# Odd layer of a nine-layer forward pass: gate products in two half units, late scans inside attention steps, rotary rows in tiles of their own

## The reference, cut to what matters

```python
def odd_mixer(h, w_in, g_cq, w_uq, g_ckv, w_ukv, conv_w, conv_b, wa, ba, wx, bx, lam, w_out):
    cq, ckv, kr, xr, xg = np.split(h @ w_in, ...)      # 256, 128, 32, 512, 512 columns
    q = (rmsnorm(cq, g_cq) @ w_uq).reshape(Bsz, S, 8, 64 + 32)
    qn, qr = q[..., :64], rope_2(q[..., 64:])
    kv = (rmsnorm(ckv, g_ckv) @ w_ukv).reshape(Bsz, S, 8, 64 + 64)
    yc = dense_mla(qn, qr, kv[..., :64], rope_2(kr), kv[..., 64:])   # full softmax attention
    yd = rglru_block(xr, xg, conv_w, conv_b, wa, ba, wx, bx, lam)
    return jnp.concatenate([yc, yd], axis=-1) @ w_out

def rglru_block(...):
    xc = conv_b + sum_j conv_w[j] * xp[:, j:j + S]     # 4 taps
    for dirn in range(2):
        r, i = sigmoid(xc @ wa[dirn] + ba), sigmoid(xc @ wx[dirn] + bx)   # block-diagonal, 64 wide
        log_a = -8 * r * softplus(-lam[dirn])
        a, b = exp(log_a), sqrt(-expm1(2 * log_a)) * (i * xc)
        h[dirn] = scan(h_t = a_t * h_{t-1} + b_t), backwards for dirn 1
    return (h[0] + h[1]) * gelu(xg)
```

## Time and profile before

| | |
|---|---|
| median of 3 runs | 2529.38 us (2527.14 to 2529.92) |
| the profiled execution | 2531.64 us, of which the span of the page 2529.8 us |
| PE busy | 2370.3 us, 94% of the span |
| DVE, ACT, POOL busy | 1318.5 us (52%), 957.7 us (38%), 280.9 us (11%) |
| odd layer, products of the first unit to the start of attention | 1869.6 to 2044.2 us |
| odd layer, attention | 2044.2 to 2112.5 us |
| loads of weight units | 184 of 1 MB, 4.8 us from issue to landing |

### The profile page before, as it was taken

One profiled execution on the slowest core, in us unless ns is written; L12 is line 12 of the kernel. 1 busy time (PEld: TensorE's weight loads), 2 busy tenths in 40 slices (PEclk: granted clock), 3 DMA queues, 4 the chain that ended last, 5 costly groups with the idle time before them and its releaser, 6 DMA issues.

```text
span 2529.8 us, 30118 instructions
## 1 busy us (share of the span) xinstructions
PE 2370.3 (94%) x11732; PEld 1867.3 (74%) x11732; DVE 1318.5 (52%) x1529; ACT 957.7 (38%) x1392; POOL 280.9 (11%) x188
## 2 busy tenths in 40 slices
PE   7999999999998989999998999999996689999997
PEld 6775667888876667888886678888875547788886
DVE  6447656664545656664647653333365565443333
ACT  3327753442322543442423533232225353332221
POOL 0000003110112003110100032110040001311010
PEclk9999999999999999999998999999998789999998
DMA  4211002222222002222232022322221101222231
GB/s 174 100 67 34 2 18 83 100 99 86 97 98 94 34 34 85 98 99 100 83 110 99 34 83 90 110 91 92 100 86 56 50 1 67 84 100 98 87 114 67
DMA packets 31202, 202.53 MB, mean 80 GB/s; under 512 B 4356, under 2 KB 5256, under 8 KB 7432
## 3 DMA queue, kind: packets, MB, share of 16 engines
q1 hardware_dynamic: 29816, 198.14, 22.2%
q10 hardware_dynamic: 1296, 3.15, 0.3%
HBM read 199.17 MB, written 2.10 MB: 80 GB/s over the span
## 4 chain that ended last, share of the span: by engine, by line
PE 83%; DVE 11%; ACT 4%; issue 1%; DMA 0%; ACTq 0%; DVEq 0%; SPq 0%
PE D L526 71%; PE X L600 3%; PE D L621 2%; PE D L613 2%; DVE neg_max L1680 2%; DVE w_lo L1475 1%; DVE xg L1509 1%; ACT prob L1177 1%; PE X L605 1%; ACT w_hi L1003 1%; DVE mid L1475 1%; DVE prob L1695 1%; ACT mid L1003 1%; PE X L717 1%; PE X L566 1%
## 5 line engine op out<-in xcount | busy, mean ns | idle before, releaser
L526 PE MATMUL D<-xg,w_hi 128*128 128x512 f32 x3184 | 1000.3, 396 | 57.1 <-DVE xg L1509 33.7
L526 PEld LDWEIGHTS D<-xg,w_hi 128*128 128x128 f32 x3184 | 604.4, 191 | 191.0 <-DVE w_lo L1475 25.7
L526 PE MATMUL D<-mid,w_hi 128*128 128x512 f32 x2312 | 719.2, 392 | 15.8 <-DVE w_lo L1475 7.7
L1475 DVE TENSOR_TENSOR w_lo<-w_raw,w_hi 128x2048 fp32r<-128x2048 f32 (+1 forms) x208 | 454.2, 2185 | 375.2 <-ACT w_hi L1003 374.9
L526 PE MATMUL D<-xg,w_lo 128*128 128x512 f32 x1592 | 626.3, 393 | 0.0
L1003 ACT ACTIVATE w_hi<-w_raw 128x2048 fp32r<-128x2048 f32 (+1 forms) x208 | 356.5, 1714 | 476.5 <-PE D L526 474.7
L526 PEld LDWEIGHTS D<-mid,w_hi 128*128 128x128 f32 x2312 | 436.3, 189 | 112.8 <-issue 17.6
L526 PE MATMUL D<-mid,w_lo 128*128 128x512 f32 x1156 | 452.2, 391 | 0.0
L526 PEld LDWEIGHTS D<-xg,w_lo 128*128 128x128 f32 x1592 | 303.3, 190 | 64.1
L526 PEld LDWEIGHTS D<-mid,w_lo 128*128 128x128 f32 x1156 | 218.7, 189 | 45.9
L1524 DVE TENSOR_TENSOR h<-D,h 128x1024 f32 (+1 forms) x72 | 88.0, 1222 | 267.8 <-PE D L526 267.8
(11 more groups left out here) (241 smaller groups left out, 1711.6 us busy)
## 6 DMA issues: line engine op xcount, KB each, us to landing
w_raw<-in_weights SPq DMA_DIRECT2D x184, 1024.0 KB, 4.8
h<-in_x SPq DMA_DIRECT2D x4, 512.0 KB, 7.9
out_y<-h SPq DMA_DIRECT2D x4, 512.0 KB, 2.7
inv_cnt<-in_inv_cnt ACTq DMA_DIRECT2D x1, 1024.0 KB, 4.9
cos<-in_cos ACTq DMA_DIRECT2D x3, 256.0 KB, 4.9
sin<-in_sin ACTq DMA_DIRECT2D x3, 256.0 KB, 5.3
vec<-in_vec SPq DMA_DIRECT2D x1, 262.0 KB, 3.0
cos<-in_cos_m ACTq DMA_DIRECT2D x1, 256.0 KB, 2.9
```

Of the source, the lines that this page charges most:

```text
L526: last = nc.tensor.matmul(out, w[a], x[b], start=start and k == 0, stop=stop and k == 2)
L1475: return nc.vector.tensor_tensor(out, x, f(high), ALU.subtract)
```

## The change

- `PHASES["odd"]`: the order becomes xr (2), cq, gates0, ckv, xg0, gates1, xg1, uq, ukv, out (4), 14 units instead of 13. `gates0` and `gates1` hold 4 gate groups each in half a unit (1024 columns); uq is 1536 columns and ukv 1024, and the splits take only these.
- ACT and DVE do the first four gate groups behind units ckv and xg0, the second four behind gates1 and xg1. The square of a is a second Exp with doubled scale on ACT (`lru_sq`), no longer a product on DVE. gelu is taken late, in place, with uq's evacuation.
- The first batch is scanned before attention; the second batch's scans, sums, gating by gelu and splits are put into attention steps 0 to 10 (`recurrence_step` on DVE, three copies on ACT).
- Queries and keys lie as in the other layers: plain rows of two heads in one tile (`mla_qn`, `mla_kn`, 64 rows a head), rotary rows in `mla_qr` (2 tiles of 4 x 32 rows) and `mla_kr`, the shared rotary key copied 4 times by the weights themselves. These four lie over `xg`. Rotation is one pass of 128 rows for the key and one for all queries. The scores are two matmuls of 64 rows and then two of 32 rows that add to the same banks.

```diff
-    "odd": (("xr", 2), ("xg", 2), ("lru", 1), ("cq", 1), ("ckv", 1), ("uq", 1), ("ukv", 1), ("out", 4)),
+    "odd": (("xr", 2), ("cq", 1), ("gates0", 1), ("ckv", 1), ("xg0", 1), ("gates1", 1), ("xg1", 1), ("uq", 1),
+            ("ukv", 1), ("out", 4)),
...
+                if kind == "odd":
+                    for o in range(2):
+                        rows = rotary_rows(t, o)
+                        last = nc.tensor.matmul(X[:, 2 * par + o, :], mla_qr[rows, t // 2, span(qt)], mla_kr[rows, :],
+                                                start=False, stop=True, skip_group_check=True)
...
+                project(at["cq"], x_norm)
+                u = at["gates0"]
+                recurrent_gates(u, 0, ((X, 0), (X, 2), (D, 2 * (u % 2)), (X, 0)))
+                project(at["ckv"], x_norm)
+                project(at["xg0"], x_norm, middle=latent_sums)
+                latent_rstd()
+                recurrent_gates(at["gates1"], 2, ((X, 0), (X, 2), (X, 0), (X, 2)))
+                project(at["xg1"], x_norm, middle=rotary_key_swap)
...
+                for n in range(6):
+                    if n >= 2:
+                        pe.wait_ge(mla_z, n - 1)
...
+                split_high(at["uq"], n=12 * P)
+                decays(1)
+                roots(1)
+                query_out(0)
+                split_high(at["ukv"], n=UNIT // 2)
+                query_out(1)
...
+                gated_inputs(0)
+                split_low(at["xg0"])
+                one_less_square(0)
...
+                split_low(at["gates1"], n=UNIT // 2)
+                both(0)
...
+                both(1)
+                split_low(at["xg1"])
+                scaled(lru_g[:, 0:2, :], at["xg0"])
...
+            def recurrence_step(s):
+
+                if s == 0:
+                    recurrence_inputs(2)
+                if s == 1:
+                    recurrence(4)
+                if s == 2:
+                    recurrence(5)
+                if s == 3:
+                    both_ways(2)
+                    gated(0)
+                if s == 4:
+                    recurrence_inputs(3)
+                if s == 5:
+                    recurrence(6)
+                if s == 6:
+                    recurrence(7)
+                if s == 7:
+                    both_ways(3)
+                    gated(1)
+                if s == 8:
+                    gated(2)
+                    gated(3)
```

More of the change, by code:

```diff
@@ L1396, in odd, with gate @@
-                for t in range(4):
-                    act.wait_ge(yd_done, t + 1)
-                    copy(mid[:, 4 + t, 0, :], lru_x[:, t, :]).then_inc(yd_high, 1)
-                split_high(at["cq"] + 1)
+                def gate(n, bank, first_bank):
+                    u = at["gates1" if n >= 4 else "gates0"]
+                    t, way, m = n // 2, n % 2, n % 4
+                    if m < 3:
+                        act.wait_ge(lru_z, n + 1 - n // 4)
+                    else:
+                        used(u)
+                    if n >= 4:
+                        act.wait_ge(lru_sum, m // 2 + 1)
+                    for g, name in enumerate(("lru_ba", "lru_bx")):
+                        c = VEC[name] + 4 * way + t
+                        ins = nc.scalar.activation(lru_ri[:, m, g, :], bank[:, first_bank + g, :], ACT.Sigmoid,
+                                                   bias=vec[:, c:c + 1])
+                        if m == 3 and g == 0:
+                            ins.then_inc(d_free[u % 2], 1)
+                    ins.then_inc(lru_gate, 1)
@@ new lines, in roots, with query_out @@
+                def roots(batch):
+                    for n in range(4 * batch, 4 * batch + 4):
+                        act.wait_ge(lru_square, n + 1)
+                        root = lru_ri[:, n % 4, 0, :]
+                        nc.scalar.activation(root, root, ACT.Sqrt).then_inc(lru_root, 1)
+                def query_out(n):
+                    u = at["uq"]
+                    if n < 5:
+                        act.wait_ge(mla_out, n + 1)
+                    else:
+                        used(u)
+                    out = mla_qr[:, n, :] if n < 2 else mla_qn[:, n - 2, :]
+                    copy(out, D[:, 2 * (u % 2) + n % 2, :],
+                         scale=float(MLA_QK) ** -0.5).then_inc(mla_z if n < 5 else d_free[u % 2], 1)
@@ L1400, in odd @@
+                split_high(at["gates0"], n=UNIT // 2)
+                conv_tap_in(1)
+                conv_high(1)
+                split_high(at["ckv"])
+                own = 2 * (at["gates0"] % 2)
+                for n, (bank, first_bank) in enumerate(((X, 0), (X, 2), (D, own), (X, 0))):
+                    gate(n, bank, first_bank)
                 act.wait_ge(d_free[at["cq"] % 2], at["cq"] // 2 + 1)
                 nc.scalar.activation(lat_sq[:, 0:2, :], lat[:, 0:2, :], ACT.Square).then_inc(lat_sqd, 1)
[L1402 removed]
+                split_high(at["xg0"])
```

484 lines of the change are left out of this document (248 added, 236 removed).

## The result

The changed kernel takes 2489.48 us (median of 4 runs, 2489.3 to 2490.78) against 2529.65 us (4 runs, 2527.14 to 2531.88) before: ratio 0.9843, 95% interval 0.9829 to 0.9857. It is faster by 40 us, where 65 were forecast and the range asked for at least 49. The profiled execution took 2489.59 us, of which the span is 2487.8.

A forecast was written before the change was run, and what follows sets the result against it. PE was taken to be bound by waits in the odd layer's projections and recurrence, and by its own work in attention. Stage 1 saves 67.2 us, attention adds 2.3: 64.9 off 2531.64 gives 2466.7, forecast 2465, range 2457 to 2480.

The forecast's parts named there:

- stage 2: Odd layer's attention: steps go from 3.82 to 4.06 us, net +2.3 us; its end and the out units stay unchanged.
- the sum: From xr1 to attention: 1880.6 + 85.5 + 0.6 + 6.0 + 2.1 + 1.0 = 1975.8, taken as 1977 us.
- Stage 1: Odd layer from xr1 to attention: waits for w_lo (18.7 us) and sigmoids (21.4) go; attention starts 67 us earlier.
- The restart at uq: Projections before attention: after the uq wait PE restarts at half clock, costing 2 us.
- The first rival: Odd layer's attention: the rotary pair does not overlap, 16 x 0.82 = 13 us more, 2478 us; chance 0.09.
- The table load: ACT ahead of uq: a switch costs 1.3 us; with the skill's added drain the time would be 2468.
- late half not hidden: Odd layer's attention: the second batch's 13.7 us on DVE move attention's end, 2479 us; chance 0.04.
- The uq wait: Before attention: PE's third uq tile waits 4.0 us until ACT evacuates the first.

The follow-up runs named there:

- the placement runs: Unused bytes behind lat_r: 32 or 384 on the kernel before, 2546.02 and 2543.28 us; 32, 96 or 352 on the changed kernel, 2479.63, 2465.69 and 2463.91 us.

## Why the prediction was wrong, and where it was right

- **The step that failed** is one sentence at the end of stage 2's working: "the end of attention and the out units stay as they are", and beside it the start of the sum, "It starts for PE at 1880.6, unchanged". All matmuls of the unedited layers were priced at nothing because no line of theirs was edited. But the change enlarges two buffers ahead of `mid`, and 3462 matmuls of nearly all layers read `mid`. Up to the odd layer the kernel is 16.2 us later and behind attention 4.2 us longer than before. Against the same kernel with 96 unused bytes, which has `mid` in a cheap place, it is 17.6 us (1896.85 - 1879.27) and 7.4 us (421.5 - 414.1). The 4.2 are fewer because the profiled kernel before has restarts at half clock behind the start of out that cost 3 us; moved as a whole by 128 bytes, it takes 414.1 us there too. No rival covered the placement. Shown by the placement runs: 24 us come back with 96 unused bytes, and 17 and 14 us can be put on the kernel before by the same means.
- **Stage 1 was right** in its mechanism, and its total, 96.5 us against 96.4, agrees partly by luck. The waits were 2.6 us at uq (4.0 forecast), 1.1 at ukv (1.3), 0.8 at the end (0.8), 0.4 for the sigmoids (0.6): 4.9 instead of 6.7. The restart at uq cost about 1.5 us (2.0 forecast). Against that, four groups of xg0 behind the latent sums, from 1944.73 to 1949.06, take 4.3 us instead of 2.7, a stretch at half clock with no wait ahead of it that the sum had at nothing, and the dear `mid` costs 0.7 here. The clock was 0.96 (over 0.95). Its argument, that splits must not stand behind the recurrence on DVE, holds by experiment for the one split that was put back: +7.7 us.
- **Attention was nearly right**: 72.9 against 70.5 us. The rotary pair costs 1.05 us rather than 1.00, as much as a 64-row pair (1.06), and transposes and values 2.05 rather than 2.00; that is 16 x 0.1 = 1.6 us of the 2.4. The rest is in what attention takes beyond its 16 steps: that was to shrink by 1.5 us and shrank by 0.8 (from 68.3 - 16 x 3.82 = 7.2 to 72.93 - 16 x 4.16 = 6.4), though the first scores now run at full clock (1.13 us for four records). That DVE idles 1.60 us in every step is true of most steps, not of all: in three of the first its idle time ahead of the maximum is 0.4 to 0.7 us; it did not matter. The first rival, an unpaired rotary product, did not happen: the rows at 2010.91 and 2011.96 put the pair at 1.05 us where 1.82 would be unpaired. The Trainium skill (TensorE: Matmul & The Clock Gate, The mechanism) lets a weight load pass a running matmul only where their row groups differ. The trace agrees as far as it goes: the rotary pair's loads start only at 2010.91, with the pair's own first matmuls. But the rule does not keep the two heads apart, as the prediction feared: their rotary rows lie in different halves of the array, and in this trace their matmuls start 0.01 us apart.
- **The table load was right**: 1.3 us again.

```profile
1971.42 0.71 ACT L1421 ACTIVATE lru_ri<-lru_ri,lru_c 128x512 f32<-128x512 f32 x1
1972.15 1.28 ACT L1427 ACT_TABLE_LOAD   x1
1973.44 2.19 ACT L1427 ACTIVATE lru_ri<-lru_ri 128x512 f32<-128x512 f32 x4
1975.54 0.57 ACT L1037 ACTIVATE mla_qr<-D 128x512 f32<-128x512 f32 x1
```

From the end of the last tanh (1972.13) to the first root (1973.44) are 1.3 us. The drain of 1.38 us that the Trainium skill (ScalarE: Activation LUTs, What ACT_TABLE_LOAD costs) counts besides does not show.
- **The rival "late half not hidden"** was priced at 2479. It did not happen, and when most of it was made to happen (the pieces of steps 0 to 7) it gave 2478.2. The price was right by accident: 13.7 us were reckoned as work, and the 12.5 came as 3 us of late work and the rest, for the most part, clock.
- **The uq wait** looked like a term that could be won back. By the runs it is worth 2 to 4 us between xr1 and attention and nothing clear of the scatter in the time; moved within ScalarE's work, it only came back at a later copy.

Added up from the rows: 16.2 later at xr1, 67.1 less to attention (163.6 - 96.5), 4.6 more in attention (72.9 - 68.3), 4.2 more behind it: -42.1 us, and the spans differ by 2529.8 - 2487.8 = 42.0.

## What to carry to other kernels

Before pricing "everything else" at nothing, look at what the edit does to the layout: any buffer that grows or appears ahead of a matmul's operand moves that operand. Keep moving operands and split weights a multiple of 256 bytes apart, the one distance that was cheap wherever it was tried here, and put small buffers of odd size behind them or round them up. When a measured gain falls short in layers that nobody edited, compare the spacing of equal matmuls before looking for a wait; a third of this change's gain hid in 0.02 us a group.

## What the runs showed of the hardware

- A 128x512 fp32 matmul at full clock costs 0.227 us (0.680 a group of three) when its moving operand lies a multiple of 256 bytes from the weights, and 0.233 to 0.234 (0.699 to 0.703) when it is 32, 128, 160 or 192 bytes off (other distances were not tried): 3% on matmuls that take most of the time. No row names it as a wait; PE shows as busy throughout. It depends on the distance, not on the address: with every buffer moved by 128 bytes a group stays at 0.680 us.
- A restart after a wait of 2.6 to 2.7 us ran at half clock for six matmuls in the changed kernel (2.7 us from 1976.17, 1.22 for the first two), and at full clock at once in the profile of the version with 96 bytes (0.73 at 1958.60). After 3.5 us early in attention, two steps of small matmuls ran at half clock. Behind the 1.8 to 1.9 us that PE waits ahead of out, the kernel before ran three groups at half clock (1.28, 1.28 and 1.07 us instead of 0.68), and none when it was moved as a whole by 128 bytes. What decides between them stays open.
